# First-product expert weights as 64-partition units of 16 KB, waited for in pairs

## What is computed

```python
def moe_ffn(h, w_router, b_router, w_gu, b_gu, w_down, b_down):
    logits = h @ w_router + b_router
    top_logit, top_idx = lax.top_k(logits, 4)        # 4 of 32 experts
    top_p = softmax(top_logit)
    for each expert e, for its tokens xb:
        gu = xb @ w_gu[e] + b_gu[e]                  # w_gu[e]: 1024 x 2048, fp32
        glu = min(gu[:, :1024], 7); lin = clip(gu[:, 1024:], -7, 7)
        act = glu * sigmoid(1.702 * glu) * (lin + 1)
        y = act @ w_down[e] + b_down[e]              # w_down[e]: 1024 x 1024, fp32
        out[token] += p * y
```

## Time and profile before

| what | value |
|---|---|
| median of three runs | 2099.54 us (2097.64 to 2106.0) |
| profiled execution, its own time | 2105.05 us |
| span of the profile | 2103.3 us |
| granted TensorE clock, mean over the span | 0.975 of full speed |
| TensorE matmul busy | 1919.1 us (91% of the span) |
| VectorE, ScalarE, GpSimd busy | 615.6, 434.7, 68.9 us |
| read from HBM | 555.02 MB |
| moved by SP's queue | 560.70 MB in 122528 packets, 67.9% of 16 DMA engines' time |

### The profile page before, as it was taken

The page is one execution under the profiler, slowest core; times in us unless marked ns, Lnnn a source line. Parts: engine busy times, 40 slices in busy tenths (PEclk is TensorE's granted clock), DMA queues, the critical chain, the costliest instruction groups (busy, mean ns, idle before and its releaser), DMA issues. The chain is left out here.

```text
span 2103.3 us, 24697 instructions
## 1 busy us (share of the span) xinstructions
PE 1919.1 (91%) x9335; PEld 1041.3 (50%) x9336; DVE 615.6 (29%) x1346; ACT 434.7 (21%) x869; POOL 68.9 (3%) x102
## 2 busy tenths in 40 slices
PE   6999997999989889999999888899999889999997
PEld 3336455887878443333333333233333245767775
DVE  1476565246620221110111111101111122432223
ACT  3222641327231111111111111001111022521011
POOL 1000400100000000000000000000000000000000
PEclk9999999899999889999999999999999999999999
DMA  9444348215373669999999999999999872114442
GB/s 360 160 167 146 139 112 200 71 49 180 117 255 140 280 264 420 421 422 422 422 422 422 422 422 422 422 422 422 422 422 422 351 276 85 68 50 152 158 156 103
DMA packets 124901, 567.15 MB, mean 270 GB/s; under 512 B 36064, under 2 KB 45024, under 8 KB 69152
## 3 DMA queue, kind: packets, MB, share of 16 engines
q1 hardware_dynamic: 122528, 560.70, 67.9%
q10 hardware_dynamic: 2304, 5.51, 0.8%
HBM read 555.02 MB, written 11.14 MB: 269 GB/s over the span
## 5 line engine op out<-in xcount | busy, mean ns | idle before, releaser
L2057 PE MATMUL expert_gb<-expert_ring,hT 128*64 128x512 f32 x768 | 203.2, 608 | 40.8 <-DMA expert_ring<-in_w_gu 39.4
L1951 DVE TENSOR_SCALAR hT<-expert_gb 128x512 f32<-128x512 f32 x32 | 22.1, 692 | 704.0 <-PE expert_lb L2057 704.0
L2057 PE MATMUL expert_lb<-expert_ring,hT 128*64 128x512 f32 x768 | 197.9, 594 | 0.0
L2105 PE MATMUL expert_yb<-expert_ring,hT 128*64 128x512 f32 x384 | 167.4, 592 | 0.0
L2105 PE MATMUL expert_yb<-expert_ring,h2T 128*64 128x512 f32 x384 | 167.4, 592 | 0.0
L469 PE MATMUL mix_in_pj<-hT,mix_in_pj_ring 128*128 128x512 f32 (+1 forms) x384 | 144.7, 536 | 1.3 <-DVE hT L589 1.3
L2463 PE MATMUL attend_bank<-hT,expert_ring 128*128 128x256 f32 x640 | 141.4, 379 | 0.0
L2463 PEld LDWEIGHTS attend_bank<-hT,expert_ring 128*128 128x128 f32 x640 | 121.6, 190 | 25.1 <-issue 9.6
L2057 PEld LDWEIGHTS expert_gb<-expert_ring,hT 128*64 128x64 f32 x768 | 46.9, 137 | 166.7 <-DMA expert_ring<-in_w_gu 115.9
L1997 ACT ACTIVATE hT<-hT 128x512 f32<-128x512 f32 x32 | 20.1, 630 | 526.0 <-DVE hT L1951 526.0
L141 PE MATMUL delta_scan_fill_bank<-hT,fill_w 128*128 128x512 f32 (+1 forms) x288 | 104.3, 522 | 8.7 <-DMA fill_w<-in_w_fill 5.9
(11 more groups left out here) (484 smaller groups left out, 2632.6 us busy)
## 6 DMA issues: line engine op xcount, KB each, us to landing
expert_ring<-in_w_gu SPq DMA_DIRECT2D x192, 1024.0 KB, 26.8
expert_ring<-in_w_down_units SPq DMA_DIRECT2D x96, 1024.0 KB, 27.1
late<-in_w_gu SPq DMA_DIRECT2D x32, 1024.0 KB, 25.9
mix_in_wm<-in_w_mod_units SPq DMA_DIRECT2D x11, 2048.0 KB, 9.6
expert_ring<-in_w_up_units SPq DMA_DIRECT2D x22, 1024.0 KB, 6.2
fill_w<-in_w_fill SPq DMA_DIRECT2D x40, 512.0 KB, 3.9
fill_w<-in_w_gu SPq DMA_DIRECT2D x16, 1024.0 KB, 26.8
ob<-in_w_gu SPq DMA_DIRECT2D x16, 1024.0 KB, 26.5
```

The source lines that it names most:

```text
L1951: v.tensor_scalar(glu, gb[j][:], LIMIT, None, ALU.min).then_inc(s_glu, 1)
L2057: m = pe.matmul(b[halves[h], :], xT[:, k, x], unit[z][:, c0 + 512 * h:c0 + 512 * h + 512], start=False, stop=(k == KT - 1))
L2105: m = pe.matmul(yb[h][halves[j], :], hidT[j][:, c, hh * SLOTS:(hh + 1) * SLOTS], unit[z][:, a * F + 512 * h:a * F + 512 * h + 512], start= ...
```

## The change

The `w_gu` units get another shape. Two neighbouring k-tiles (256 rows of `w_gu`) are a pair of units. The first unit of the pair holds, for both k-tiles, the rows that go to partitions 0 to 63, the second those for partitions 64 to 127; so each is 64 partitions of 16 KB, still 1 MB. The host lays the array out so (`w_gu_halves`), contiguous per unit. The pair fills the same two slots as before. Slots 14 and 15 are tiles apart from each other, so there a unit is two transfers of 64 partitions by 8 KB, and, since the semaphores of these two slots now get 32 per use, the `w_down` units in them are also split in two transfers of 128 partitions by 4 KB. TensorE waits, ahead of the first k-tile of a pair, for both units of the pair. SP waits until both slots of a pair are given back before it loads the first. In `merge_route_stage` unit 15 is now loaded behind unit 14, and unit 12 together with 13 after `s_xs`. The products, their number and their order stay.

```diff
+++ merge_route_stage, SP
                 sp.wait_ge(S.fill.done, F1)
-                load_expert_unit(sp, A, S, 0, 15, 15)
                 sp.wait_ge(s_pa, 2)
                 load_expert_unit(sp, A, S, 0, 14, 14)
+                load_expert_unit(sp, A, S, 0, 15, 15)
                 for n in range(8, 12):
                     load_expert_unit(sp, A, S, 0, n, n)
                 sp.wait_ge(s_y, 1)
                 for n in range(4):
                     load_expert_unit(sp, A, S, 0, n, n)
                 sp.wait_ge(s_t, 4)
-                for n in (4, 5, 6, 7, 12):
+                for n in range(4, 8):
                     load_expert_unit(sp, A, S, 0, n, n)
                 sp.wait_ge(s_xs, 2)
-                load_expert_unit(sp, A, S, 0, 13, 13)
+                for n in (12, 13):
+                    load_expert_unit(sp, A, S, 0, n, n)
+++ load_expert_unit
-    dst = S.unit[z]
     if u < 2 * KT:
-        e, n = pair * 2 + u // KT, u % KT
-        src = A.w_gu[bass.ds(e, 1), n * P:(n + 1) * P, :].rearrange("e p n -> (e p) n")
+        e, n, half = pair * 2 + u // KT, u % KT // 2, slice(64 * (u % 2), 64 * (u % 2) + 64)
+        src = A.w_gu_halves[bass.ds(e, 1), n, u % 2].rearrange("e p n -> (e p) n")
+        first = z - u % 2
+        if first == 14:
+            for k in range(2):
+                sp.dma_start(S.unit[first + k][half], src[:, 2 * D * k:2 * D * (k + 1)]).then_inc(S.landed[z], 16)
+            return
+        wide16 = S.late if first == 12 else S.ring[:, first:first + 2]
+        sp.dma_start(wide16[half].rearrange("p a n -> p (a n)"), src).then_inc(S.landed[z], 16)
+        return
     else:
+        dst = S.unit[z]
         e, n = pair * 2 + u % 2, (u - 2 * KT) // 2
         src = A.w_down_units[bass.ds(e, 1), n].rearrange("e p n -> (e p) n")
+    if z >= 14:
+        for k in range(2):
+            sp.dma_start(dst[:, D * k:D * (k + 1)], src[:, D * k:D * (k + 1)]).then_inc(S.landed[z], 16)
+        return
     sp.dma_start(dst, src).then_inc(S.landed[z], 16)
+++ expert_stage, SP (the same in all three loops)
-                            sp.wait_ge(s_used, (p * PAIRS + i * 2) * PER + (n + 1))
+                            sp.wait_ge(s_used, (p * PAIRS + i * 2) * PER + (n + 2 - n % 2))
+++ expert_stage, TensorE
                 def arrived(it, n, odd):
-                    return it * PER + (16 * ((PER // 3 * odd + n) // RING + 1) - PER // 3 * odd)
+                    times = 2 if slot(n, odd) >= 14 else 1
+                    return it * (times * PER) + times * (16 * ((PER // 3 * odd + n) // RING + 1) - PER // 3 * odd)
...
-                            pe.wait_ge(landed[z], arrived(it, u, odd))
+                            if k % 2 == 0:
+                                for w in (u, u + 1):
+                                    pe.wait_ge(landed[slot(w, odd)], arrived(it, w, odd))
+++ layouts
-        "w_gu": f(x["w_gu"][0]), 
+        "w_gu_halves": f(x["w_gu"][0].reshape(NE, KT // 2, 2, 2, 64, 2 * D).transpose(0, 1, 3, 4, 2, 5)
+                         .reshape(NE, KT // 2, 2, 64, 4 * D)), 
```

More of the change, by code:

```diff
@@ L1882, in body @@
                         for n in range(RING, RING + 2 * PER):
-                            sp.wait_ge(s_used, (p * PAIRS + i * 2) * PER + (n + 1))
+                            sp.wait_ge(s_used, (p * PAIRS + i * 2) * PER + (n + 2 - n % 2))
                             load_expert_unit(sp, A, S, i * 2 + n // PER, n % PER, n % RING)
                     for n in range(RING, 2 * PER):
-                        sp.wait_ge(s_used, p * (PAIRS * PER) + ((PAIRS - 2) * PER + n + 1))
+                        sp.wait_ge(s_used, p * (PAIRS * PER) + ((PAIRS - 2) * PER + n + 2 - n % 2))
                         load_expert_unit(sp, A, S, PAIRS - 2 + n // PER, n % PER, n % RING)
@@ L1889, in body @@
                         for n in range(RING):
-                            sp.wait_ge(s_used, p * (PAIRS * PER) + (PAIRS * PER + n + 1))
+                            sp.wait_ge(s_used, p * (PAIRS * PER) + (PAIRS * PER + n + 2 - n % 2))
                             load_expert_unit(sp, A, S, 0, n, n)
```

## The result

The changed kernel takes 2813.83 us (median of four runs, 2786.77 to 2909.77), beside 2098.59 us for the kernel before on the same chip: a ratio of 1.3345, 95% interval 1.3272 to 1.3417. Ratios and intervals in this document leave out the runs that are more than 1.5% above the fastest of their kernel (here the one of 2909.77 us); the medians have them in. The forecast was 2638 us with a range of 2086 to 2730 us: the direction was right, and the slowdown of 715 us was larger than the 538 us forecast, and the time lies 84 us beyond the upper end of the range.

A forecast was written before the change was run, and what follows sets the result against it. The prediction took the expert stage to be bound by its DMA bytes. From the profiled 2105.05 us, + 528 (`w_gu` shape) + 9 (first units) + 1 (slots 14, 15) gave 2643, 2638 us on the runs' scale; range 2086 to 2730 us.

The forecast's parts named there:

- What bounds the kernel: Expert stage: all 16 DMA engines busy at 420 GB/s for 919 us; the stage ends when its bytes have come.
- Part 1, the factor: `w_gu` transfers to 64 partitions: engines share a way in, factor 2.0, so 5.0 us a unit for 2.50.
- The rival that the halves run side by side: DMA queues in the stream: engines a unit apart, or eight engines per transfer, avoid sharing; 2089 to 2095 us, chance 0.28.
- Part 1, the relief: `w_gu` stream: engines some 1 us apart share less, 0.3 us off a unit, leaving 2.2 us excess, +528 us in all.
- The bound without any relief: `w_gu` stream with full sharing: 240 x 2.5 = +600 us, the upper bound of part 1.
- Part 2, the first 16 units: First `w_gu` loads from 690 us: they take 75 us, gaps close, the stream begins 9 us later; bounds 0 and +20.
- Part 3: Slots 14 and 15: `w_down` in 4 KB runs costs +1 us; `w_gu` there adds no bytes, SP's 46 extra transfers hidden.
- Part 4, the waits: TensorE's and SP's waits for both units or slots of a pair: cost 0, covered by 11 units in flight.
- Part 5, the clock: TensorE's clock may fall with longer waits; 79 us against 95 us of transfers a pair of experts, hidden, 0.
- What would show it: Expert stage, if right: share near 1, 210 to 230 GB/s for `w_gu`, 420 for `w_down`, stream ending near 2200 us.
- A share under 0.9 would put the loss in waits or in the issue: Expert stage, sign that the forecast is wrong: DMA share under 0.9 there means the loss is in waits or issue.

The follow-up runs named there:

- the waits alone: The changed kernel's waits, order of loads and SP rule, with the old transfers of 128 partitions by 8 KB: 2103.99 us, ratio 1.001.
- short rows: The kernel before, each `w_gu` unit as two transfers of 64 partitions by 8 KB, `w_down` as two of 4 KB rows: median 2608.01 us.
- the run of 2562.62 us: The changed kernel, upper half loaded first, one DMA engine given 64 KB of copies ahead of the stream: 2562.62 us, its other run 2779.23 us.
- the kernel kept in step: The changed kernel, with SP waiting once a pair of experts until everything issued has landed, then a tiny copy: 2763.62 us, ratio 1.3143.

## Why the prediction was wrong, and what in it was right

The direction and the cause of the slowdown were right, and the time was missed by 176 us, because the part on the relief had the engines' drift wrong.

**What bounds the kernel: right.** The stream's bytes set the end of the expert stage before and after; the stretch behind it is 428 us in both.

**Part 1, the factor: right, and shown as the cause.** 4.91 us a unit at a full share was measured, 5.0 forecast from the 32-partition rows. That the shape alone does it is shown: taking it away leaves 1.001 (the waits alone), keeping only it brings 2351 to 2655 us (short rows), and every second partition in place of neighbours takes the whole loss away. The rival that the halves run side by side did not hold in either of its forms. A transfer that used only eight engines would have left the next one the other eight; but 214 GB/s come with all 16 busy (100.7%). And eight engines about a unit behind the others are as slow. Something of that rival is in the run of 2562.62 us, but it came to 303 GB/s, not to 400.

The Trainium skill's page "SBUF — State Buffer", section "Door 1: The DMA port swizzle (why `[64,N]` ≈ `[32,N]`)", gives 196 GB/s for 64 neighbouring partitions. The 213 GB/s here agree with its direction and nearly with its size. Its table of ports would let partitions 32 to 95 reach all 16 ports, and so run at full rate. The first transfers of that kernel agree (309 ns for 8 KB); in the stream behind them there are 212 GB/s, and the measurement decides.

**Part 1, the relief: the step that failed.** The forecast took 0.3 us a unit off, 240 x 0.3 = 72 us, because engines get out of step by some 1 us and those that are ahead run dry and start together with the others again. They did not start together again: the distance between the first and the last engine grew from 7 to 45 us. The 16 KB packets became 4% shorter than in step (1190 for 1241 ns), which gave 43 us. What the step left out is the other side of the same drift. It took `w_down` at its old 2.50 us and the share at 1, and neither held: 76 us of disturbed `w_down` packets, and 72 us more of engine time left over than before. A term of -72 us was in truth one of +105 (76 + 72 - 43). The bound without any relief, +600, had the same gap, so the end of the range was too low as well. That drift makes the disturbed packets and the empty engines is shown by the kernel kept in step: its distance is 0.4 us, its `w_down` packets are back at 314 ns, and the 37 us that it leaves over are about what its stops cost.

**Part 2, the first 16 units: right.** The gaps closed as foreseen (208 GB/s from 714 to 723 us, where there was nothing). Of these units all but 144 packets of 16 KB, 2.25 units, had come by 756 us; at 4.96 us each they put 11 us on the stream, where 9 were forecast.

**Part 3.** The `w_down` units with 4 KB rows take 163 ns for half a packet of 314, so 16 units x 256 x 6 / 16 = +1.5 us, as forecast. `w_gu` in slots 14 and 15, counted like the others, costs more: if the 14336 packets of the 112 `w_down` units take 314 ns in the kernel kept in step, its other 3840 of 8 KB take 672, 5.38 us a unit, 12 us over 30 units.

**The sum again**, for the stream of the profiled execution, with the unit times of the table: 240 x (4.96 - 2.51) = 588, less 43 of relief, + 11 (first units), + 12 and + 1.5 (slots 14 and 15), + 76 (`w_down`), + 3 (the smallest packets), + 72 (left over) makes 720.5, where it grew by 1639 - 919 = 720 us.

**Part 4, the waits: right.** 1.001 for them alone. **Part 5, the clock: right.** It fell to 0.78 to 0.84, and TensorE still waited 332.2 us for `w_gu`; behind the stream the 428 us are unchanged.

**What would show it.** The rate with `w_gu` (some 215), with `w_down` (403 to 423) and on average up to 1500 us (255), the doubled time to landing and the waits of several us one a pair came as written. The average of the whole stream did not (237 GB/s for about 260), nor did its end (2395 us for near 2200). "A share under 0.9 would put the loss in waits or in the issue" was wrong too: at 0.89 it was fifteen engines that had run ahead of one.

**What stays open.** Which resource 64 neighbours share. That the first middle units came at full rate speaks for a limit in each half of the partitions. But then eight engines a unit behind the others, in the other half, should have been relieved, and were not. Distances of half a unit and a unit for one engine did not bring relief about at the start either; other distances and other sets of engines were not tried.

## What to carry to other kernels

In a stage whose bytes set its end, give every transfer all 128 partitions, or spread the fewer ones over them: a slice of 64 neighbours within one half cost a factor of two here, with the DMA share near 1, so that only the GB/s beside it tells. Once that is so, rows of 16 KB in place of 8 KB gain a little, 0.5% of this kernel. When one kind of transfer in a queue is slow, price what it does to those behind it as well. A unit has landed only with its slowest part, so look at how far apart a transfer's 16 steps come: 4 us went with a gain here, 45 us with a loss.

## What was not expected of the hardware

- 64 partitions with a step of two run at the full 426 GB/s (614 ns for 16 KB), 64 neighbours in one half at 213 (1190 to 1241 ns). Partitions 32 to 95 begin at full rate (309 ns for 8 KB, 616 for 16 KB) and are slow in the stream (212 GB/s).
- The limit on such transfers loosens at times: one kernel gave 2351 and 2655 us, another 2563 and 2779; every kernel whose transfers use all partitions agrees within 0.6%.
- DMA engines that serve one queue drift apart, by a median of 45.6 us from 1800 to 2100 us; the last unit's last step came 27.8 us behind its first.
- Copies of 8 neighbouring rows of 16 KB from HBM to HBM go over all 16 engines in 8 KB packets; with rows that are not neighbours only eight engines took part.
